# A two-layer encoder trunk on one core: one-hot tiles ahead of the weight subtraction, attention units with a later value product in column halves

## What is computed

```python
# layer 0, attention; two head groups of one projection
sa = einsum('bmqd,bmkd->bmqk', qa, ka) * scale + bias      # 8 maps of 64, relative bias
pa = softmax(sa).reshape(B, 4, 2, Q, S)
oa = einsum('bhqk,bhkd->bhqd', pa[:,:,0] - lam * pa[:,:,1], va)   # 4 heads, values 128 wide
sb = einsum('bgrqd,bgkd->bgrqk', qb, kb) * scale           # 8 query heads, 2 key/value heads
ob = einsum('bgrqk,bgkd->bgrqd', softmax(sb), vb)          # values 64 wide
y = concat(rms_norm(oa, subln_g) * (1 - lambda_init), ob) @ w_out

# both layers, expert block: 8 heads, top 16 of 128 x 128 keys, 16384 experts
s = einsum('thpc,hpnc->thpn', h @ w_q, subkeys)
eidx, gate = top 16 of the pair sums, softmax over them
act = gelu(einsum('thkd,td->thk', u_tab[eidx], h))
y = einsum('thk,thkd->td', gate * act, v_tab[eidx])
```

## Time and profile before

| | us |
|---|---|
| median of 3 runs | 5050.2 (5049.36 to 5051.71) |
| the profiled execution | 5053.89 |
| its span | 5052.1 |
| TensorE busy | 4698.1 (93%) |
| VectorE busy | 2459.9 (49%) |
| ScalarE busy | 1544.1 (31%) |
| mean granted TensorE clock | 0.975 of full |

### The profile page before, as it was taken

How to read it: one execution, slowest core, us unless ns; L and a number is a source line. 1 busy time by engine, 2 the same in 40 slices (tenths; PEclk the granted TensorE clock), 3 DMA queues, 4 the chain that set the end, 5 groups by cost and what they waited for, 6 DMA issues and landing times. The chain is left out here.

```text
span 5052.1 us, 64351 instructions
## 1 busy us (share of the span) xinstructions
PE 4698.1 (93%) x24100; PEld 3730.1 (74%) x24100; DVE 2459.9 (49%) x4117; ACT 1544.1 (31%) x2178; POOL 313.1 (6%) x169
## 2 busy tenths in 40 slices
PE   6977799999999999989699999988999999999999
PEld 2434588777888888844499999956877778888887
DVE  5633595555234555540456555526955541344444
ACT  1122333333222222210344333413333332222222
POOL 0000233000000000000300000003420000000000
PEclk9899999999999999989799999998999999999999
DMA  5300234555656666522300000012445556555553
GB/s 227 107 1 34 75 119 154 173 201 173 208 186 234 224 225 225 206 86 103 130 18 25 24 18 22 1 50 92 129 161 175 199 175 208 168 194 199 187 199 133
DMA packets 248143, 690.90 MB, mean 137 GB/s; under 512 B 12920, under 2 KB 78712, under 8 KB 239904
## 3 DMA queue, kind: packets, MB, share of 16 engines
q1 hardware_dynamic: 240544, 654.99, 38.1%
q0 software_dynamic: 7424, 33.56, 1.8%
HBM read 533.27 MB, written 155.22 MB: 136 GB/s over the span
## 5 line engine op out<-in xcount | busy, mean ns | idle before, releaser
L1296 DVE TENSOR_TENSOR pe_lo<-pe_raw,pe_hi 128x2048 fp32r<-128x2048 f32 x222 | 508.9, 2292 | 1360.2 <-ACT pe_hi L1076 1360.2
L771 PE MATMUL bank<-pe_hh,pe_hi 128*128 128x512 f32 x2304 | 914.5, 397 | 51.4 <-POOL pe_lo L1174 48.9
L773 PE MATMUL bank<-pe_hh,pe_lo 128*128 128x512 f32 x2304 | 900.2, 391 | 0.0
L772 PE MATMUL bank<-pe_hl,pe_hi 128*128 128x512 f32 x2304 | 899.5, 390 | 0.0
L771 PE MATMUL bank<-pe_ah,pe_hi 128*128 128x512 f32 x2048 | 796.7, 389 | 0.0
L772 PE MATMUL bank<-pe_al,pe_hi 128*128 128x512 f32 x2048 | 796.7, 389 | 0.0
L773 PE MATMUL bank<-pe_ah,pe_lo 128*128 128x512 f32 x2048 | 796.7, 389 | 0.0
L1076 ACT ACTIVATE pe_hi<-pe_raw 128x2048 fp32r<-128x2048 f32 x272 | 520.5, 1913 | 588.4 <-PE bank L773 580.1
L771 PEld LDWEIGHTS bank<-pe_hh,pe_hi 128*128 128x128 f32 x2304 | 434.0, 188 | 140.6 <-POOL pe_lo L1174 51.2
L773 PEld LDWEIGHTS bank<-pe_hh,pe_lo 128*128 128x128 f32 x2304 | 433.8, 188 | 92.0
L772 PEld LDWEIGHTS bank<-pe_hl,pe_hi 128*128 128x128 f32 x2304 | 434.4, 189 | 85.4
(11 more groups left out here) (281 smaller groups left out, 5655.7 us busy)
## 6 DMA issues: line engine op xcount, KB each, us to landing
pe_raw<-in_stream SPq DMA_DIRECT2D x272, 1024.0 KB, 5.7
acts<-h SPq DMA_DIRECT2D x128, 512.0 KB, 7.6
gates<-pe_stage SPq DMA_DIRECT2D x32, 2048.0 KB, 7.4
pe_w<-gates SPq DMA_DIRECT2D x32, 2048.0 KB, 10.2
h<-acts SPq DMA_DIRECT2D x128, 512.0 KB, 4.1
ada_ring<-in_ada_w SPq DMA_DIRECT2D x32, 768.0 KB, 7.1
at_ada_ring<-in_ada_w POOLq DMA_DIRECT2D x16, 1024.0 KB, 7.7
rwkv_proj<-rp_out POOLq DMA_DIRECT2D x64, 256.0 KB, 2.7
```

The source lines that it names most:

```text
L771: nc.tensor.matmul(out, left[0], right[0], start=start, stop=False)
L772: nc.tensor.matmul(out, left[0], right[1], start=False, stop=False)
L773: return nc.tensor.matmul(out, left[1], right[0], start=False, stop=stop)
L1296: nc.vector.tensor_tensor(lo[:, side], raw[:, side], hi[:, side].bitcast(F32), ALU.subtract).then_inc(low, 1)
```

## The change

It has four parts. In the gate loop both slots' one-hot tiles are made, and then the weights' low part. In the attention units the value product stands one iteration later (`attend(u - 2)`, ahead of the transposes `turn(u - 1)`), the two 64-row products of kind A stand side by side behind both bias products, and the value product of kind B writes two halves of 64 output partitions from `vhead` (64 columns a head, no padding), each kc's two halves in turn. The sum of the modulation moves from the end of the first block to the start of the output block, where the means and the `w_out` products of the first four chunks alternate; `w_out` is loaded during the units. In the first block the first weight load stands ahead of the small loads, and the relative rows are made behind the first projected chunk.

Buffers: `ada_acc` now lives through the whole stage; `bucket` and `relrow` only through its first block.

```diff
@@ sync, first block
-                sp.dma_start(bucket[:, :], io["bucket"]).then_inc(small_loaded, 16)
-                sp.dma_start(relb[:, :], io["rel_bias"]).then_inc(small_loaded, 16)
...
                     sp.dma_start(wt[:, m % WR], io["w_in"][m]).then_inc(w_loaded[m % WR], 16)
+                    if m == 0:
+                        sp.dma_start(bucket[:, :], io["bucket"]).then_inc(small_loaded, 16)
+                        sp.dma_start(relb[:, :], io["rel_bias"]).then_inc(small_loaded, 16)
+                        sp.dma_start(lam_in[:, :, :].rearrange("p a b -> p (a b)"),
+                                     io["lam"].to_broadcast([P, 4 * HD])).then_inc(small_loaded, 16)
@@ tensor, first block
                     last.then_inc(projected, 1)
+                    if m == 0:
+                        relative_rows()
...
-                pe.wait_ge(std_done, QK_CHUNKS)
-                pe.wait_ge(ada_accumulated, len(ADA_TILES))
-                sum_modulation(K, ada_acc, ada_summed, bank=3, first=EARLY // P, n=48 - EARLY // P)
@@ vector, first block
-                nc.vector.memset(vpad[:, :, :, :], 0.0).then_inc(prepared, 1)
...
-                        nc.vector.tensor_copy(vpad[:, :, 0, 0:HD], vb[:, :, 0, :]).then_inc(v_copied, 1)
-                        nc.vector.tensor_copy(vpad[:, :, 1, HD:P], vb[:, :, 1, :]).then_inc(v_copied, 1)
+                        nc.vector.tensor_copy(vhead[:, :, :, :], vb).then_inc(v_copied, 1)
...
-                finish_modulation(K, dve, 0, ada_summed, mod_done, bank=3, first=EARLY // P, n=48 - EARLY // P, subs=(1,))
+                dve.wait_ge(ada_accumulated, len(ADA_TILES))
@@ units
+            @block.sync
+            def _(sp):
+                for m in range(WR):
+                    sp.dma_start(wt[:, m], io["w_out"][m]).then_inc(wo_loaded[m], 16)
...
-                    if u >= 2:
+                    if u >= 2 and kind == "B":
                         pe.wait_ge(exped, 2 * (u - 1))
+                    if kind == "A":
+                        for e in range(2):
+                            if u >= 2:
+                                pe.wait_ge(exped, 2 * (u - 2) + e + 1)
+                            nc.tensor.matmul(banks[e], K.const("anti"), toep[:, 2 * a + e, off:off + T], start=True,
+                                             stop=False)
                     for e in range(2):
...
+                        nc.tensor.matmul(banks[e], qkv[rows[e], q, qs], qkv[rows[e], k, :], start=(kind == "B"),
+                                         stop=True).then_inc(scored, 1)
+
+                def turn(u):
...
+                def attend(u):
+                    kind, a, qb = UNITS[u]
                     if u >= 2:
                         pe.wait_ge(head_copied, u - 1)
...
+                    pe.wait_ge(p_copied, tiles_before(u + 1))
+                    out = K.ps[6 + u % 2]
+                    for kc in range(TC):
+                        if kind == "A":
+                            last = nc.tensor.matmul(out[:, 0:P], vtok[:, kc, a, :], probT[:, u % 2, 0, kc, :],
+                                                    start=(kc == 0), stop=(kc == TC - 1))
+                        else:
+                            for e in range(2):
+                                last = nc.tensor.matmul(out[HD * e:HD * (e + 1), 0:P], vhead[:, kc, e, :],
+                                                        probT[:, u % 2, e, kc, :], start=(kc == 0), stop=(kc == TC - 1))
...
-                for u in range(len(UNITS)):
-                    scores(u)
-                    if u:
-                        attend(u - 1)
-                attend(len(UNITS) - 1)
+                N = len(UNITS)
+                for u in range(N + 2):
+                    if u < N:
+                        scores(u)
+                    if u >= 2:
+                        attend(u - 2)
+                    if 1 <= u <= N:
+                        turn(u - 1)
@@ output block
+                finish_modulation(K, dve, 0, ada_summed, mod_done, bank=6, first=EARLY // P, n=48 - EARLY // P, subs=(1,))
                 for m in range(DC):
                     dve.wait_ge(wo_done, m + 1)
...
+                sum_modulation(K, ada_acc, ada_summed, bank=6, first=EARLY // P, n=48 - EARLY // P)
+                for m in range(WR):
+                    mean_of(m)
+                    pe.wait_ge(wo_loaded[m], 16)
+                    project(m, 4, DC)
+                for m in range(DC):
+                    if m >= WR:
+                        pe.wait_ge(wo_loaded[m % WR], 32)
+                        pe.wait_ge(added, m - 3)
+                        project(m, 4, DC)
+                    project(m, 0, 4).then_inc(wo_done, 1)
@@ gate loop, vector
                     for e in range(4):
-                        make_hot(8 * i + 2 * e, 0, 64 * i + 16 * e)
+                        for half in range(2):
+                            make_hot(8 * i + (2 * e + half), half, 64 * i + (16 * e + 8 * half))
                         make_low(4 * i + (FIRST_GATED + e + 1), 1 - e % 2)
-                        make_hot(8 * i + (2 * e + 1), 1, 64 * i + (16 * e + 8))
```

More of the change, by code:

```diff
@@ L332, in stage_attention @@
         vtok = K.sb(ctx, "at_vtok", [P, TC, 4, P])
-        vpad = K.sb(ctx, "at_vpad", [P, TC, 2, P])
+        vhead = K.sb(ctx, "at_vhead", [P, TC, 2, HD])
         toep = K.sb(ctx, "at_toep", [P, MAPS, TOEP_W])
@@ L411, in _, with relative_rows @@
             def _(pe):
-                pe.wait_ge(small_loaded, 48)
-                for half in range(2):
-                    nc.tensor.matmul(K.ps[6 + half][0:MAPS, :], relb[:, :], bucket[:, half * T:(half + 1) * T],
-                                     start=True, stop=True).then_inc(rel_done, 1)
+                def relative_rows():
+                    pe.wait_ge(small_loaded, 48)
+                    for half in range(2):
+                        nc.tensor.matmul(K.ps[6 + half][0:MAPS, :], relb[:, :], bucket[:, half * T:(half + 1) * T],
+                                         start=True, stop=True).then_inc(rel_done, 1)
                 def mean_of(m):
@@ L562, in stage_attention @@
         head_copied = K.sem("at_head_copied")
+        wo_loaded = [K.sem(f"at_wo_loaded{i}") for i in range(WR)]
         def tiles_before(u):
@@ L602, in attend @@
                         last.then_inc(p_transposed, 1)
+                def attend(u):
+                    kind, a, qb = UNITS[u]
                     if u >= 2:
                         pe.wait_ge(head_copied, u - 1)
-                    out = K.ps[6 + u % 2][:, 0:P]
-                    for e in range(n):
-                        pe.wait_ge(p_copied, tiles_before(u) + e + 1)
-                        for kc in range(TC):
-                            v = vtok[:, kc, a, :] if kind == "A" else vpad[:, kc, e, :]
-                            last = nc.tensor.matmul(out, v, probT[:, u % 2, e, kc, :], start=(e == 0 and kc == 0),
-                                                    stop=(e == n - 1 and kc == TC - 1))
+                    pe.wait_ge(p_copied, tiles_before(u + 1))
[8 more added lines that the diff above has]
+                                                        probT[:, u % 2, e, kc, :], start=(kc == 0), stop=(kc == TC - 1))
                     last.then_inc(attended, 1)
                 pe.wait_ge(toep_loaded, 16)
-                for u in range(len(UNITS)):
-                    scores(u)
-                    if u:
-                        attend(u - 1)
-                attend(len(UNITS) - 1)
+                N = len(UNITS)
[6 more added lines that the diff above has]
+                        turn(u - 1)
             @block.scalar
@@ L688, in stage_attention @@
         sub_normed = K.sem("at_sub_normed")
-        wo_loaded = [K.sem(f"at_wo_loaded{i}") for i in range(WR)]
         wo_done = K.sem("at_wo_done")
@@ L694, in _ @@
             def _(sp):
-                for m in range(DC):
-                    if m >= WR:
-                        sp.wait_ge(wo_done, m - WR + 1)
+                for m in range(WR, DC):
+                    sp.wait_ge(wo_done, m - WR + 1)
                     sp.dma_start(wt[:, m % WR], io["w_out"][m]).then_inc(wo_loaded[m % WR], 16)
@@ L728, in _, with mean_of @@
             def _(pe):
-                for a in range(4):
+                def mean_of(a):
                     pe.wait_ge(sub_squared, a + 1)
@@ L734, in _, with project @@
                                      stop=True).then_inc(sub_meaned, 1)
-                for m in range(DC):
-                    pe.wait_ge(wo_loaded[m % WR], 16 * (m // WR + 1))
-                    if m >= 4:
-                        pe.wait_ge(added, m - 3)
-                    for i, k in enumerate((4, 5, 6, 7, 0, 1, 2, 3)):
+                def project(m, first, end):
+                    for k in range(first, end):
                         if m == 0 and k < 4:
```

32 lines of the change are left out of this document (11 added, 21 removed).

## The result

The changed kernel takes 4861.3 us (median of 4 runs, 4859.8 to 4864.1) against 5049.8 us before: 0.963 of the time, 95% interval 0.961 to 0.964. The forecast was 4864 us.

The account below looks back on a forecast made before the run. TensorE, busy 93% of the span, was taken as the bound: its work plus its waits. Savings of 73.5 + 99 + 8.7 + 1 + 4 = 186 us gave 4864 us against the 5050.2 median; range 4845 to 4910.

Parts of the forecast that it names:

- Gate loop: One-hot products: tiles made before `pe_lo` remove TensorE's stall, a pair falling from 14.03 to 12.88 us; -73.5 us.
- The check by pitch: Gate loop: stall taken from the pair's period, 14.03 against 12.88 us without stall, so 1.15 us a pair.
- the group's idle time (61): Gate loop: TensorE's idle time in front of `pe_hot`, the other bound on the saving, -61 us.
- Kind A: First 16 attention units: period from 7.32 to 4.3 us, TensorE the bound; 48 us saved.
- Kind B: Second 16 attention units: period from 5.91 to 3.4 us, VectorE the bound; 40 us saved, or 27 without overlap.
- Rival (a): Second-kind units: column halves run one after the other, 4.2 us a unit, +13 us, 4877 us; chance 0.14.
- The clock in the units: Attention units: 125 us at full rate plus 11 us half-rate cost (3 to 30), loop 136 us, -99 us.
- Rival (b): Attention units: clock stays at half for 40% of the loop, 180 instead of 136 us, +44, 4908 us; chance 0.12.
- The modulation sum: Moved to the output stage: units begin 8.7 us earlier; output stage -1 us (-2 to +3), products covering the means' waits.
- The start: Projection start: weights issued first, first product near 61.5 instead of 67.14, less two small groups; -4 us (-1 to -6).
- Rivals (c) to (e): (c) gate stall half removed, 4901, 0.07; (d) gate loops lose clock, 5276, 0.02; (e) steps stay 14.03, 4938, 0.05.

Follow-up runs that it names:

- padded values: Changed kernel with kind B's values padded to 128 columns again, so whole-array value products, still one iteration later: 4870.5 us, 9.2 us more.
- the product at once: Changed kernel with the value product back in the same iteration as its transposes, behind them: 4943.7 us, 82 us more.

## Why the prediction was right, and where it was not

The time is inside both ranges, 3 us from the forecast. Its terms fit less well than the sum: the output block came 5 us worse than forecast and the units 8 us better, nearly all of it by their clock, so that so small a miss is in part luck.

- **Gate loop: right.** Forecast -73.5, measured -70.8 in the loops of the changed kernel, and as much in the loops of the run that changes nothing else (its whole time, 4978.1, is 76 us below the 5054.0 that ran beside it; what is over lies outside the loops). The difference to the forecast is 12.92 against 12.88 us a pair. The check by pitch was the right bound, the group's idle time (61) the wrong one: it counts from a modelled end, and showed 0.95 us for a stall that by pitch cost 1.12 (14.04 less 12.92). `pe_lo` comes when it came before, relative to its step, as was said.
- **Kind A: right.** 4.30 us forecast and measured, TensorE the bound, VectorE waiting 0.55 us for its scores.
- **Kind B: right in mechanism, 0.15 us too long.** 3.25 us for 3.4, since the guess put a gap between VectorE's units that is not there. The halves take 1.02 us for the 1.1 assumed. Rival (a), halves one after the other, falls: the passes of the two halves start 0.04 us apart in the changed kernel, where each half alone follows itself at 0.11 us, and their weight loads run under the running products. The rule of the Trainium skill, "TensorE: Matmul & The Clock Gate", Part 3, that such loads overlap only when the row group differs, does not agree with this trace. The rival's price was set at 13 us; the nearest run, padded values, has 9.
- **The clock in the units: mis-sized.** 11 us of half-rate cost were assumed, bounds 3 and 30. One half-rate stretch is left, 4.6 us at the start of the units. It cost 2.2 us: the same units without it, in the run with six more VectorE operations, take 126.0 us from the first score to the end of the last value product, and 128.2 here. (The 126.0 stand against 125 forecast at full rate: kind B is 2 us shorter in all, the ends are 3 us longer.) This stretch begins at 206.1, 2.3 us ahead of the units and with no one-column product near; that the first microseconds would still follow idle time was said. Rival (b), a clock that stays down, falls: TensorE's waits and the half-rate stretches went together, and the run with the product at once brings both back together. The rival's price was also miscounted: 125 x 1.67 is 209 and not 180, and 125 us of work in a loop that is at half rate for 40% of its time take 125 / 0.8 = 156 us, 20 us over the sum's 136 and not 44.
- **The modulation sum: the step that failed.** The -8.7 us came as said, at the first scores. But the step took the sum for 7.5 to 9.5 us in its new place and the block for as long as before, -1 us, at most +3; it is +4.2, since the sum takes 11.8 us (337.14 to 348.94) and the mean and the products behind it run at half rate for 3.9 us more. What the runs show in its place: in a row of their own, or in two rows of 32 passes, the 64 passes cost 12 to 14 us in each of the four places tried in the changed kernel, with the clock at half for a part of them or all, and for what follows. In three of these it falls 2 to 5 us after they have begun, with dense work in front or not; at the end of the first block it had fallen 1.1 us earlier, and there the sum only ran through it. The move is then worth nothing (4862.1 and 4861.3 us); worth 8.9 us is what the step saw as mere cover, the means among the products. Why the clock falls in such a row, no run shows.
- **The start: right, low by 2.** -6.2 for -4, just outside its bound of -6 (5.7 in the run with the start undone); the first weights landed 3.7 us after their issue (55.05 to 58.76) where the median of all loads, 6.0, was taken.
- Rivals (c) to (e) fall with the gate loop's numbers: no wait, 12.92 us, clock 1.00.

## What to carry to other kernels

Where two producers take turns on one engine, price each order by who waits for which product and when: a tile that is wanted half a step later can cost a stall in each step while the engine that makes it is half idle. Take a copy between engines out of the line of the engine that is the bound, by an iteration's lag, before the products are made cheaper: here the lag was worth 83 us, side-by-side scores 20, column halves 9, each undone alone in the changed kernel. Products with one column don't belong in a row of their own; spread among dense products they cost about half as much here (7.2 us for 13.1).

## What the runs showed of the hardware

- 64 one-column passes in a row took 9.5, 11.9, 13.7 and 9.4 us in four places, each time with the granted clock at half from 2 to 5 us after their start or already before it, and up to 22 us beyond their end (the kernel before, 217.4 to 244.8); at full clock 32 of them took 3.56 us. As 16 groups of four between dense products they took 0.36 us a group, with the clock at full.
- The clock also falls without them: in the changed kernel it is at half from 206.1 to 212.9, while TensorE waits between the transposes at the end of the first block.
- Two column halves of 64, with float32 weights loaded for each product, run side by side: 16 passes in 1.02 us against 1.89 for as many on the whole array. With the two halves' products not alternating in the code, they still overlapped in part: 1.51 us.
- A bias and a 64-row product in turn cost about 1.03 us each, two bias products then two 64-row products 2.87 us together in place of 4.1; by estimate 0.75 us of the saving is the overlap (two 64-row products in 1.06 us, two whole-array ones in 1.81), and the rest, some 0.5 us, fewer changes of the array's shape, which no run tried alone.
